# Head norms and the first tiles' transposes of an output projection moved into attention jobs

## What is computed

```python
def _merge(oa, of, subln_g, lam_init, w_o):
    oa = _rmsnorm(oa, subln_g) * (1.0 - lam_init)       # per diff head, 128 columns
    o = jnp.concatenate([oa.reshape(B, S, -1), of.reshape(B, S, -1)], axis=-1)
    return o @ w_o                                      # 1024 x 1024

xp = xp + _rmsnorm(_merge(oa, of, ...), attn_post_g)    # x2 below
h = _rmsnorm(x, pre_g)
g = h @ w_gate                                          # 1024 x 2816
u = h @ w_up
... conv of width 3 on g, gelu(c) * u, @ w_down, sandwich norm
```

## Time and profile before

| what | value |
|---|---|
| three runs | 1519.66, 1523.64, 1526.92 us (median 1523.64) |
| profiled execution: its own time | 1524.37 us |
| profiled execution: span | 1522.5 us |
| granted TensorE clock, mean | 0.985 |
| PE busy / share of the span | 1443.3 us / 95% |
| last instruction of attention ends (POOL) | 654.99 us |
| first product of the output projection | 664.85 us |
| first product in the FFN's block | 800.24 us |

### The profile page before, as it was taken

How to read it: one execution, slowest core, us unless ns; L and a number is a source line. 1 busy time by engine, 2 the same in 40 slices (tenths; PEclk the granted TensorE clock), 3 DMA queues, 4 the chain that set the end, 5 groups by cost and what they waited for, 6 DMA issues and landing times. The chain is left out here.

```text
span 1522.5 us, 26842 instructions
## 1 busy us (share of the span) xinstructions
PE 1443.3 (95%) x10412; PEld 1293.5 (85%) x10412; DVE 848.3 (56%) x1375; ACT 636.9 (42%) x1192; POOL 373.9 (25%) x548
## 2 busy tenths in 40 slices
PE   7999899999999898779999999999999999999998
PEld 6999776777777676467769999999999999999998
DVE  6412566466553444444457776667766646444573
ACT  6723655444344344353332532333333325343543
POOL 5223876764544540042230000000000000000120
PEclk9999999999999999989999999999999999999999
DMA  5213557577767565412123122222222236655773
GB/s 182 57 34 98 167 167 216 181 224 225 236 188 222 185 190 169 126 58 73 66 85 92 56 84 84 84 79 75 84 70 71 84 105 221 200 189 180 230 267 111
DMA packets 174832, 209.91 MB, mean 138 GB/s; under 512 B 22051, under 2 KB 118891, under 8 KB 174668
## 3 DMA queue, kind: packets, MB, share of 16 engines
q1 hardware_dynamic: 174706, 208.21, 43.7%
HBM read 178.37 MB, written 29.88 MB: 137 GB/s over the span
## 5 line engine op out<-in xcount | busy, mean ns | idle before, releaser
L575 POOL TENSOR_TENSOR k_page<-k_page,q_bc 128x256 f32<-128x256 f32 x256 | 186.7, 763 | 139.2 <-DMA k_page<-in_cache_fox_k 106.0
L1107 PE MATMUL PS<-ht_hi,w_hi 128*128 128x344 f32 x576 | 196.3, 341 | 6.5 <-POOL w_lo L546 3.4
L1107 PE MATMUL PS<-ht_hi,w_lo 128*128 128x344 f32 x576 | 186.8, 324 | 0.0
L1107 PE MATMUL PS<-ht_lo,w_hi 128*128 128x344 f32 x576 | 186.7, 324 | 0.0
L2298 PE MATMUL PS<-act_hi,wd_hi 128*128 128x344 f32 x528 | 169.1, 320 | 2.4 <-DVE act_lo L2136 2.4
L2298 PE MATMUL PS<-act_hi,wd_lo 128*128 128x344 f32 x528 | 168.6, 319 | 0.0
L2298 PE MATMUL PS<-act_lo,wd_hi 128*128 128x344 f32 x528 | 168.5, 319 | 0.0
L793 ACT ACTIVATE probs<-probs,stat 128x256 f32<-128x256 f32 (+7 forms) x128 | 98.8, 773 | 129.5 <-DVE stat L1011 128.8
L2133 DVE TENSOR_TENSOR wd_lo<-wd_raw,wd_hi 128x1024 fp32r<-128x1024 f32 (+1 forms) x88 | 87.8, 1000 | 113.2 <-ACT act_hi L1947 93.1
L1107 PEld LDWEIGHTS PS<-ht_hi,w_hi 128*128 128x128 f32 x576 | 110.8, 192 | 32.2 <-issue 24.6
L1944 ACT ACTIVATE wd_hi<-wd_raw 128x1024 fp32r<-128x1024 f32 (+1 forms) x88 | 74.3, 845 | 142.0 <-DMA act_raw<-a_dram 104.1
(11 more groups left out here) (259 smaller groups left out, 3301.1 us busy)
## 6 DMA issues: line engine op xcount, KB each, us to landing
wd_raw<-in_w_down SPq DMA_DIRECT2D x44, 512.0 KB, 3.6
k_page<-in_cache_diff_k SPq DMA_DIRECT2D x64, 256.0 KB, 2.9
k_page<-in_cache_fox_k SPq DMA_DIRECT2D x64, 256.0 KB, 3.2
v_page<-in_cache_diff_v SPq DMA_DIRECT2D x64, 256.0 KB, 2.8
v_page<-in_cache_fox_v SPq DMA_DIRECT2D x64, 256.0 KB, 3.0
w_raw<-in_w_in SPq DMA_DIRECT2D x24, 512.0 KB, 5.0
a_dram<-conv SPq DMA_DIRECT2D x22, 516.0 KB, 3.1
act_raw<-a_dram SPq DMA_DIRECT2D x66, 172.0 KB, 3.8
```

The costliest lines, as they stand in the source:

```text
L575: ins = pool.tensor_tensor(kpage[:, g % 2, c:c + PIECE], kpage[:, g % 2, c:c + PIECE], qbc[:, c:c + PIECE], ALU.mult)
L1107: ins = pe.matmul(PS[0:rows, z_bank(c), 0:THIRD], b[:, k, :], a[:, k, third(i)], start=(k == 0 and p == 0), stop=(k == KC - 1 and p == 2))
```

## The change

- **Head norms in attention jobs.** For prompt tile v the four squares are made by ACT at the end of job 35 + 5v//2 (35, 37, 40, 42, 45, 47, 50, 52), the rstd by POOL in the next job and the scaling by DVE in the one after. `g_sub` is loaded by SP in job 33. Only the sample's head norm stays in merge.
- **Two tiles turned in attention.** In jobs 57, 59, 61 and 62 PE turns a half of tile 0 or 1 (four transposes into bank 6), ACT makes hi right behind the exponentials, DVE lo at the job's end.
- **Two weight rows split in attention:** ACT in job 59, DVE in job 60. To make room `wo_hi` of each row has its own place, and the sample's scratch (`z_new`, `o_all` and others) lies in free token columns of `ht_hi` and `ht_lo`.
- **merge's order** is 0, 1, 2, 3, sample, 4, 5, 6, 7. Tiles 0 and 1 are made together: weight row as outer loop for rows 0 to 3 (48 products), then tile 0's other 24, turn of tile 2, tile 1's other 24. For the others the turn of the tile comes first, then 24 products, turn_h of two before, 24 products. On ACT and DVE the hi and lo of h come last in each step.
- **The sample's product** has hi (8 columns), 24 zeros and lo (8) as one stationary operand of 40 columns: 32 products in place of 48. ACT copies rows 32 to 39 of the result, DVE adds them to rows 0 to 7. The product with `w_lo` covers hi and lo alike.
- **The end:** turn_h(7), 48 gate products, turn_h(8), 48 up products (f = 0, i = 0 and 1 each). Their weights are loaded after the last tile's turn, and split by ACT and by DVE (no longer POOL). The FFN's block leaves out these 96.

In the code after, L1729 is a product, L1737 one of the sample, L1716 a transpose of merge, L1488 an FFN product, L832 exponentials, L847 the hi of a turned tile in attention, L897 the hi of a weight row, L1395 the transpose of the last output.

```diff
+    norm_job = lambda v: 4 * NT + 3 + 5 * v // 2
+    turn_jobs = {NJ - 7: (0, 0), NJ - 5: (1, 0), NJ - 3: (0, 1), NJ - 2: (1, 1)}
...
             # POOL, attention job J
+            def head_stat(v):
+                c = slice(HEADS * (v % 4), HEADS * (v % 4) + HEADS)
+                pool.wait_ge(a_sq, HEADS * (v + 1))
+                pool.tensor_scalar(a_st[:, 1, c], a_st[:, 0, c], 1.0 / P, EPS, ALU.mult, ALU.add).then_inc(a_step, 1)
+                pool.wait_ge(a_step, v + 1)
+                pool.tensor_tensor(a_st[:, 2, c], a_st[:, 1, c], a_st[:, 3, c], ALU.pow).then_inc(a_rstd, 1)
...
                 if J < NJ:
                     exponentials(J)
+                if J in turn_jobs:
+                    turned_hi(*turn_jobs[J])
                 chunks(before)
...
+                for v in range(NT):
+                    if norm_job(v) == J:
+                        head_squares(v)
+                if J == NJ - 5:
+                    act.wait_ge(io["wo_in"], 16)
+                    act.wait_ge(red_done, DB * PAGES)
+                    for k in range(EARLY_ROWS):
+                        act.activation(wo_hi[k][:, :], wo_raw[:, k, :], ACT.Copy).then_inc(w_hi_done_o, 1)
...
+            def head_norm(v):
+                dve.wait_ge(a_rstd, v + 1)
+                for k in range(HEADS):
+                    dve.scalar_tensor_tensor(row, row, a_st[:, 2, c:c + 1], g_sub[:, :], ALU.mult, ALU.mult).then_inc(a_norm, 1)
...
+                for v in range(NT):
+                    if norm_job(v) + 2 == J:
+                        head_norm(v)
+                if J in turn_jobs:
+                    turned_lo(*turn_jobs[J])
+                if J == NJ - 4:
+                    for k in range(EARLY_ROWS):
+                        dve.tensor_tensor(wo_lo[:, k, :], wo_raw[:, k, :], wo_hi[k][:, :].bitcast(F32), ALU.subtract).then_inc(w_lo_done_o, 1)
...
+            def turn_attention(v, half):
+                pe.wait_ge(a_norm, HEADS * NT)
+                for k in range(4):
+                    ins = pe.transpose(PS[:, 6, k * P:(k + 1) * P], qo[:, 4 * half + k, v * P:(v + 1) * P], ident[:, :])
+                ins.then_inc(t_done, 1)
...
             # PE, merge
+            pe.wait_ge(t_lo, 2 * IN_JOBS)
+            for k in range(KC // 2):
+                pe.wait_ge(w_lo_done, k + 1)
+                for s in range(2):
+                    for half in range(2):
+                        product(s, half, k)
+            for s in range(2):
+                for k in range(KC // 2, KC):
+                    pe.wait_ge(w_lo_done, k + 1)
+                    for half in range(2):
+                        ins = product(s, half, k)
+                ins.then_inc(b_done, 1)
+                if s == 0:
+                    turn_a(2)
+            for s in range(2, NS):
+                if s + 1 < NS:
+                    turn_a(s + 1)
+                pe.wait_ge(t_lo, a_batch[s] + 2)
+                pe.wait_ge(y_scaled, s - 1)
+                if s == SAMPLE:
+                    turn_h(s - 2)
+                    for k in range(KC):
+                        ins = sample_product(k)
+                else:
+                    for k in range(KC):
+                        product(s, 0, k)
+                    turn_h(s - 2)
+                    for k in range(KC):
+                        ins = product(s, 1, k)
+                ins.then_inc(b_done, 1)
+            turn_h(NS - 2)
+            pe.wait_ge(t_lo, h_batch[ORDER.index(2 * THIRD // P)] + 2)
+            for up in range(2):
+                pe.wait_ge(y_scaled, NS - 1 + up)
+                pe.wait_ge(gu_lo, weight_parts(0, up))
+                for i in range(2):
+                    ffn_product(pe, PS, (GATE_BANKS, UP_BANKS)[up][i], w_ffn_hi, w_ffn_lo, ht_hi, ht_lo, 0, up, i)
+                if not up:
+                    turn_h(NS - 1)
...
             # PE, ffn
-                    if f == 0 and not up and i < 2:
+                    if f == 0 and i < 2:
                         continue
```

More of the change, by code:

```diff
@@ L488, in _ @@
                         load_value_page(g)
+                if u == 4 and t == 1:
+                    sp.dma_start(g_sub[:, :], io["subln_g"].to_broadcast([P, P])).then_inc(sub_in, 16)
                 if u == 3 and t == 2:
@@ L1462, in _ @@
+                if s >= 1:
+                    u = s - 1
                     sp.wait_ge(x2_done, u + 1)
[L1463 to L1465 removed]
+                    sp.dma_start(io["x2_dram"][tokens(u), :], x2[0:rows(u), u % 2, :]).then_inc(x2_stored[u % 2], 16)
+            for n in range(2):
+                sp.wait_ge(x2_stored[n], 16 * ((NS + 1 - n) // 2))
@@ L1501, in _ @@
+            pool.wait_ge(a_sq, HEADS * NS)
+            rstd(DB, *(a_st[0:DB, q, 0:HEADS] for q in range(4)), P, a_rstd)
+            for u in range(NS):
+                n = rows(u)
+                for c, width, squared, done in ((Y + u % 2, D, y_sq, y_rstd), (X + u % 2, D, x2_sq, x2_rstd)):
+                    pool.wait_ge(squared, u + 1)
+                    rstd(n, *(st[0:n, q, c:c + 1] for q in range(4)), width, done)
         @block.scalar
         def _(act):
-            b = 0
-            def hi(t):
+            b = 2 * IN_JOBS
@@ L1506, in hi @@
+            def hi(s, sample=False):
                 nonlocal b
-                n = rows(t)
+                n = rows(s)
                 for half in range(2):
@@ L1570, in lo @@
+                    dve.tensor_tensor(low, src, high.bitcast(F32), ALU.subtract).then_inc(t_lo, 1)
                     b += 1
-            def norm_attn(v):
-                n = rows(v)
-                dve.wait_ge(a_rstd, v + 1)
-                for k in range(4):
-                    c = A + 4 * (v % 4) + k
-                    head = attn(v, k)
-                    dve.scalar_tensor_tensor(head, head, st[0:n, 2, c:c + 1], g_sub[0:n, :], ALU.mult, ALU.mult).then_inc(a_norm, 1)
-            dve.wait_ge(sub_in, 16)
@@ L1600, in _ @@
+            dve.wait_ge(a_rstd, NS)
+            for k in range(HEADS):
+                row = attn(SAMPLE, k)
+                dve.scalar_tensor_tensor(row, row, a_st[0:DB, 2, k:k + 1], g_sub[0:DB, :], ALU.mult, ALU.mult).then_inc(a_norm, 1)
+            dve.wait_ge(consts_in, 32)
+            for s in range(1, NS + 2):
+                u = s - 1
+                if u < NS:
                     m = rows(u)
+                    if u == SAMPLE:
+                        dve.wait_ge(y_copied, 1 + 1)
+                        dve.tensor_tensor(y_samp[0:DB, :], sample_y[0:DB, :], y_samp[0:DB, :], ALU.add).then_inc(y_copied, 1)
@@ new lines, in turn_a, with turn_h, product @@
+            def turn_a(s):
+                turn(s, lambda c: attn(s, c))
+            def turn_h(s):
+                pe.wait_ge(h_done, s + 1)
+                turn(s, lambda c: h[0:rows(s), c * P:(c + 1) * P])
+            def product(s, half, k):
+                for n, (a, w) in enumerate(((ht_hi, w_hi[k]), (ht_hi, w_lo[:, k, :]), (ht_lo, w_hi[k]))):
+                    ins = pe.matmul(PS[:, 2 * (s % 2) + half, :], a[:, k, tokens(s)], w[:, half * 512:half * 512 + 512],
+                                    start=(n == 0 and k == 0), stop=(n == 2 and k == KC - 1), skip_group_check=True)
+                return ins
@@ new lines, in sample_product @@
+            def sample_product(k):
+                for n, w in enumerate((w_hi[k], w_lo[:, k, :])):
+                    for half in range(2):
+                        c = slice(512 * half, 512 * half + 512)
+                        ins = pe.matmul(sample_y[0:LO_AT + DB, c], stacked[:, k, :], w[:, c],
+                                        start=(n == 0 and k == 0), stop=(n == 1 and k == KC - 1), skip_group_check=True)
+                return ins
+            pe.wait_ge(t_lo, 2 * IN_JOBS)
[4 more added lines that the diff above has]
+                        product(s, half, k)
```

315 lines of the change are left out of this document (158 added, 157 removed).

## The result

The changed kernel took 1514.43 us (median of seven runs, 1509.19 to 1517.54) against 1522.95 for before (seven runs, 1519.66 to 1526.92): a ratio of 0.9941, interval 0.9918 to 0.9964. On another chip, in the experiments, it was 1515.96 against 1525.61, ratio 0.9932 (0.9909 to 0.9955). So it is 8 to 10 us faster, where 22 were forecast, and outside the range of 1496.5 to 1510.

A forecast was written before the change was run, and what follows sets the result against it. It took TensorE (PE), busy 95% of the span, as the bound. Merge −17.1, FFN block −7.3 and attention +2.2 sum to −22.2 us, from 1524.37 to 1502.2, given as 1502.0; range 1496.5 to 1510.

The forecast's parts named there:

- The start of merge: Start of the out projection: PE makes its first product at 655.45, right at the block's start, with operands and weight rows ready.
- the 1.6 us for the clock: Start of the out projection: 1.6 us lost to PE's lower clock, taken from a span of 0.9 to 2.0.
- the tie: End of merge: h(8) is ready at 773.65, when PE reaches the last turn_h too; 0.3 us taken for it.
- The weight rows, the full tiles and the sample: Merge: weight rows stay ahead of PE, five full tiles take 64.0 us, the sample 9.05 with its transposes.
- Rival (b): Clock stays low from the out projection's start to 668.9: 6.8 us lost, not 1.6, giving 1507; chance 0.06.
- The FFN block: FFN block: 48 up products leave, −7.5 us; 0.2 back at f = 1, wait for g_rows stays; −7.3 in all.
- The last unit: Attention's last unit: ACT's hi ahead of the row copies costs 1.3 us, from 0 to 2.4; other moved work hidden.
- rival (a): Attention exposes more, by DVE and POOL blocking each other or ACT's and DVE's last-unit work: 1506 to 1510; chance 0.15.
- rival (d): Slower: moved work, 38.4 us, lands on attention's chain through in-order queues and dependent jobs: 1538; chance 0.05.
- between 0 and 9.1 I take a tenth, 0.9: Attention's eight norm jobs: DVE's moved norms, 9.1 us, cost PE only 0.9, as DVE idled 3.4 a wait there.
- The collision: Attention: DVE's head norms and POOL's page multiplies block each other on shared SBUF ports; 5.2 us late, 1507, if all meet.
- My remark that few meet: Attention: few head norms meet a POOL page multiply, since POOL was busy 83.6 of 186 us.

## Why the prediction failed, point by point

**The start of merge** was right. The first product came at the block's start; the 1.6 us for the clock were 0 in the first profile and 0 to 3.1 in the others. From the first product to the FFN's block I had 127.7 us; it took 125.8, in others up to 128.7 with the clock low for a while; 1.6 of the difference is that clock term, 0.3 the tie. The weight rows, the full tiles and the sample held, as did the tie at the last turn_h, with no wait seen. Rival (b) did not come.

**The FFN block** was right in its work and wrong in its sum: 63.6 to 59.1 us, so 4.5 for 7.3, since the clock fell behind the wait for g_rows (granted 0.57 from 795 to 803 in the windows above) and took 3.4. Before it did not fall there. PE came to f = 1 13.9 us into the block, 10.5 without that loss, where I had 10.9.

**The last unit** was right: ahead of PE's last attention instruction it took 653.38 − 585.08 = 68.3 us before, 3.4 of them clock, and 661.59 − 596.58 = 65.0 after, with none. That is 0.1 of work, for the 1.3 that I took. PE's last attention instruction ended at 661.59, above the 660 that was to be the sign of rival (a) or (d), but that was lost in units 4 to 6.

**Units 4 to 6 failed**, and there the step "between 0 and 9.1 I take a tenth, 0.9". Its end of 9.1 was DVE's norms alone, and it was compared with a mean: DVE idled 3.4 us a wait. Those 18 waits are also of all the jobs from 400 to 586 us, not of the eight norm jobs as I wrote. The term measured 17.5. Three things went wrong in it. First, ACT was left out. I counted 9.9 us of squares, not the reads of the accumulator beside them, which have a row of their own in the same view of before:

```profile
L1522 ACT ACTIVATION_READ_ACCUMULATOR head_squares<-q_t 128x1 f32 x32 | 6.0, 189 | 0.0
```

and although these rows overlap the squares', a tile's four squares and four reads hold ACT 1.7 us, where I had 1.24. And I never asked what stands behind them in its queue. It is the next a_t, for which PE was already waiting in before (0.9 us at L1293): at the end of a job ACT had no slack, ahead of a job's exponentials it idled 0.7 to 3.6 us in before. That was 7.1 us. Second, a mean idle time says nothing of a seam. Where a unit ends, DVE is behind PE: none of the 18 waits of rows 10 lies there, and PE was waiting for L997 in before already (2.8 us in two waits). That tile 0 gives PE little to do ahead of it is my reading, not tested. The two norms that stand there were on the path in full, the other six not at all: 3 to 4 us. Third, I priced the clock where it had been low and not where the change would make new waits: 6.7 us, more than a third of the loss. Rival (a) had the right kind of cost but looked for it in the collision and in the last unit, and ended at 1510; rival (d) had the right mechanism, at all of 38.4 us.

**The collision** was real, in part. The norms' row and the reads' in 400 to 600 us after:

```profile
L1094 DVE SCALAR_TENSOR_TENSOR q_t<-q_t,head_stat,g_sub 128x128 f32<-128x128 f32 x32 | 13.7, 490 | 0.1
...
L843 ACT ACTIVATION_READ_ACCUMULATOR head_squares<-q_t 128x1 f32 x32 | 6.0, 188 | 0.0
```

13.7 us for 9.1 in merge. Five of the eight groups took 1.13 us, three 2.52 to 3.00, beside a multiplication on POOL. The Trainium skill ("SBUF — State Buffer", "SBUF: two separate sides") says that of two such instructions, one on VectorE with two inputs in SBUF and one on GpSimd that reads SBUF, the one that starts first has the shared ports for its whole length and the other is fully blocked. For DVE the trace agrees: 3.00 us for its four instead of 1.13. For POOL it does not: its four took 2.91 us instead of 2.77, and both together 3.06, where one after the other would be 2.77 + 1.13 = 3.90. And in the earlier trace rows L1616, the one held up, started 0.03 us ahead of POOL's split, and took 3.45 us where one after the other is 2.34 + 1.27 = 3.61. My remark that few meet was right too, three in eight, and it cost under 2 us each; one of the three stood at a seam, and off the seams it cost PE nothing.

**Chances.** 0.95 for faster by over 0.5% came true by a hair (0.59%, with an interval from 0.36%). The range was too narrow on the slow side, since a case between (a) and (d) had no place in it. Its lower end, by its own terms (2.2 of attention, 0.7 of clock and 3.6 of spread under 1502.0), should have been 1495.5.

## What to carry to other kernels

When work is put into another stage, read for each engine what stands directly behind the new instructions in its queue and whether PE waits for that already, job by job; a mean of idle time covers seams where there is none. The same holds for work that is moved on PE: the constants' transposes, once late, held a copy on DVE and with it the next weights. The place for such work is ahead of a wait that the engine has anyway: moving the same instructions to such a place took the gain from 10 to 22 us. And where a change makes new waits of 1 to 6 us on a busy PE, its clock is a term of the sum; cutting two traces at the same work, with the clock's share beside each piece, shows it at once.

## What the runs showed of the hardware

- Each square of ACT that also sums is followed by a read of the accumulator, a row of its own of 0.188 us. The rows overlap in part: four squares with their reads hold ACT 1.7 us, where the four squares' rows come to 1.24.
- The clock fell behind PE's waits inside stretches where PE is busy 90% and more. In units 4 to 6 of the 13 profiles it fell 31 times, each time within a wait of PE of 1.4 us or more or less than 1.6 us after its end; eight waits of 1.5 to 2.4 us had no fall behind them.
- Its loss per execution was 13.3 to 27.6 us in the profiled ones, and executions of one kernel differ mostly with it. The untouched first 411 us took 405.5 with 3.4 of it and 413.5 with 12.0. Of 21 executions of the kernel before, that with the highest mean clock (0.992) took 1516.67 us and that with the lowest (0.982) 1532.16.
- A stationary operand of 40 columns costs a product as much as one of 8 or 128 does: after, 32 products of the sample in 7.5 us, 0.234 each; before, those of 8 columns started every 0.23 us, and the full tiles' every 0.2335.
